# Reading the dense products' columns in woven lines of 16, with operands at new places modulo 512 bytes

## What is computed

```python
def first_block(x, ...):
    h = rmsnorm(x, attn_norm_w)                  # 256 x 1024
    proj = h @ w_in                              # 1024 x 3072
    y = group_rmsnorm(mixers(proj))
    x = x + y @ w_out                            # 1024 x 1024
    g = rmsnorm(x, ffn_norm_w)
    return x + (silu(g @ w_gate) * (g @ w_up)) @ w_down      # d_ff 2816

def second_block(x, ...):
    proj = rms_norm(x, mix_norm_g) @ w_in
    merged = gates0 * (y_a @ w_branch_a) + gates1 * (y_b @ w_branch_b)
    x = x + merged @ w_out
    up = rms_norm(x, ffn_norm_g) @ w_up
    a = causal_depthwise_conv(up[..., :2816], conv_w, conv_b)
    return rms_norm(x + (gelu(a) * up[..., 2816:]) @ w_down, final_norm_g)
```

## The kernel before

| tile | before | after the change |
| --- | --- | --- |
| `raw0`, `raw1`, `raw2` | 128 | 128 |
| `whi0`, `wlo0` | 128 | 128 |
| `whi1`, `wlo1` | 128 | 192 |
| `whi2`, `wlo2` | 128 | 256 |
| `hx` | 128 | 128 |
| `yx` | 160 | 320 |
| `G` | 128 | 128 |

## Time and profile before

### The profile page before, as it was taken

One profiled execution on the slowest core, in us unless ns is written; L12 is line 12 of the kernel. 1 busy time (PEld: TensorE's weight loads), 2 busy tenths in 40 slices (PEclk: granted clock), 3 DMA queues, 4 the chain that ended last, 5 costly groups with the idle time before them and its releaser, 6 DMA issues.

```text
span 689.2 us, 10065 instructions
## 1 busy us (share of the span) xinstructions
PE 681.6 (99%) x4120; PEld 601.0 (87%) x4120; DVE 498.7 (72%) x690; ACT 400.7 (58%) x503; POOL 9.3 (1%) x25
## 2 busy tenths in 40 slices
PE   9999999999999999999999999999999999999996
PEld 8889999888888888888878888899988888888885
DVE  6875777979986766766665477687779988886453
ACT  7875856755555544464467465564557666665342
POOL 1000000003000000000000000000000000000000
PEclk9999999999999999999999999999999999999999
DMA  8853325655565555545434346454555555554611
GB/s 328 337 224 123 117 70 182 222 184 192 184 217 184 201 184 184 186 181 193 175 126 179 123 150 217 153 183 155 184 200 197 192 179 189 193 197 174 222 61 61
DMA packets 19773, 124.05 MB, mean 180 GB/s; under 512 B 2320, under 2 KB 3472, under 8 KB 5520
## 3 DMA queue, kind: packets, MB, share of 16 engines
q1 hardware_dynamic: 18432, 120.07, 49.0%
q10 hardware_dynamic: 1296, 3.35, 1.4%
HBM read 122.36 MB, written 1.05 MB: 179 GB/s over the span
## 4 chain that ended last, share of the span: by engine, by line
PE 91%; DVE 4%; ACT 3%; issue 1%; DVEq 0%; POOL 0%; ACTq 0%; POOLq 0%
PE psum L1628 35%; PE psum L1629 18%; PE psum L1621 10%; PE psum L1622 10%; PE psum L1623 10%; PE psum L1617 2%; DVE wlo L985 2%; ACT whi L530 2%; PE psum L1972 1%; PE psum L2103 1%; PE psum L1671 1%; PE psum L1674 1%; PE psum L1677 1%; PE psum L2151 0%; DVE gates L1522 0%
## 5 line engine op out<-in xcount | busy, mean ns | idle before, releaser
L985 DVE TENSOR_TENSOR wlo<-raw,whi 128x2048 fp32r<-128x2048 f32 x110 | 251.6, 2290 | 75.3 <-ACT whi L530 75.3
L530 ACT CAST whi<-raw 128x2048 fp32r<-128x2048 f32 x110 | 209.7, 1908 | 43.4 <-PE psum L1623 38.1
L1628 PE MATMUL psum<-hx,whi 128*128 128x512 f32 x528 | 184.2, 395 | 0.0
L1629 PE MATMUL psum<-hx,wlo 128*128 128x256 f32 x528 | 146.7, 278 | 0.0
L1628 PE MATMUL psum<-yx,whi 128*128 128x512 f32 x352 | 123.2, 392 | 1.0 <-DVE yx L1001 1.0
L1628 PEld LDWEIGHTS psum<-hx,whi 128*128 128x128 f32 x528 | 99.0, 188 | 23.3 <-issue 0.2
L1629 PEld LDWEIGHTS psum<-hx,wlo 128*128 128x128 f32 x528 | 99.3, 188 | 0.0
L1629 PE MATMUL psum<-yx,wlo 128*128 128x256 f32 x352 | 99.2, 282 | 0.0
L1628 PEld LDWEIGHTS psum<-yx,whi 128*128 128x128 f32 x352 | 66.1, 188 | 15.3 <-DVE yx L1001 1.6
L1629 PEld LDWEIGHTS psum<-yx,wlo 128*128 128x128 f32 x352 | 66.5, 189 | 0.0
L1628 PE MATMUL psum<-G,whi 128*128 128x512 f32 x176 | 61.1, 394 | 0.0
(11 more groups left out here) (273 smaller groups left out, 1106.3 us busy)
## 6 DMA issues: line engine op xcount, KB each, us to landing
raw<-in_stream SPq DMA_DIRECT2D x110, 1024.0 KB, 4.8
raw<-in_stream SPq DMA_DIRECT2D x8, 256.0 KB, 5.3
relb<-in_relb ACTq DMA_DIRECT2D x1, 1536.0 KB, 7.4
raw<-in_stream SPq DMA_DIRECT2D x2, 512.0 KB, 7.4
x<-in_xT SPq DMA_DIRECT2D x3, 256.0 KB, 5.1
out_t<-sq SPq DMA_DIRECT2D x4, 160.0 KB, 2.4
final_gain<-in_final_gain ACTq DMA_DIRECT2D x1, 512.0 KB, 4.8
bsp<-in_bsp ACTq DMA_DIRECT2D x1, 384.0 KB, 3.4
```

The source lines that it names most:

```text
L530: act.copy(whi[s][:], raw[s][:]).then_inc(unit_hi, 1)
L985: dve.tensor_tensor(wlo[s][:], raw[s][:], whi[s][:], ALU.subtract).then_inc(unit_lo, 1)
L1628: pe.matmul(bank[b][:], stat[0], mov, start=first, stop=False, skip_group_check=True)
L1629: return pe.matmul(bank[b][:, 0:T], stat[1], mov[:, 0, :], start=False, stop=last, skip_group_check=True)
```

## The change

Three things change. No instruction is added, removed or moved on any engine: the built programs have 3970 matmuls each, and as many instructions on DVE, ACT, POOL and SP.

First, the dense matmuls read their streamed columns, and write PSUM, in another order. `woven` turns an access to 512 columns (two halves of 256) into 16 rounds of 16 columns of the first half and 16 of the second: columns 0 to 15, 256 to 271, 16 to 31, 272 to 287, and so on. 256 columns are read the same way as two halves of 128 in 8 rounds. The destination is walked in the same order, so each column's sum goes where it went before. Sixteen fp32 columns are 64 bytes. The halves begin 1024 bytes apart (512 bytes for 256 columns). In the last unit, pieces of 384 and 128 columns stay as they were.

Second, the allocation order is another one, with three pads of 64 bytes, so that the weights' three places lie at 128, 192 and 256 modulo 512, `hx` at 128 and `yx` at 320.

Third, `LEAD` is 112 in place of 160, which makes up for the pads: `G` and `gates` stay where they were.

```diff
-LEAD = 160
+LEAD = 112
...
         raw = [sb(f"raw{s}", [P, UNIT]) for s in range(RING)]
-        whi = [sb(f"whi{s}", [P, UNIT], F32R) for s in range(RING)]
-        wlo = [sb(f"wlo{s}", [P, UNIT], F32R) for s in range(RING)]
-
-
+
+
+        whi, wlo = [None] * RING, [None] * RING
+
+        def place(s):
+            whi[s] = sb(f"whi{s}", [P, UNIT], F32R)
+            wlo[s] = sb(f"wlo{s}", [P, UNIT], F32R)
+
+        hx = sb("hx", [P, KT, 2, T], F32R)
+        place(0)
+        sb("before_second", [P, 16])
+        place(1)
+        sb("before_third", [P, 16])
+        place(2)
+        sb("before_yx", [P, 16])
+        yx = sb("yx", [P, KT, 2, T], F32R)
         sq = sb("sq", [P, KT, T])
-        hx = sb("hx", [P, KT, 2, T], F32R)
...
-        yx = sb("yx", [P, KT, 2, T], F32R)
...
+            def woven(ap):
+
+                if len(ap.shape) == 3:
+                    return ap.rearrange("p h (j c) -> p j h c", c=16)
+                if ap.shape[1] % UF:
+                    return ap
+                return ap.rearrange("p (h j c) -> p j h c", h=2, c=16)
+
+            def woven_matmul(dst, stat, mov, **kw):
+                return pe.matmul(woven(dst), stat, woven(mov), **kw)
+
             def three(dst, stat, mov, first, last, **kw):
 
-                pe.matmul(dst, stat[0], mov[0], start=first, stop=False, **kw)
-                pe.matmul(dst, stat[0], mov[1], start=False, stop=False, **kw)
-                return pe.matmul(dst, stat[1], mov[0], start=False, stop=last, **kw)
+                woven_matmul(dst, stat[0], mov[0], start=first, stop=False, **kw)
+                woven_matmul(dst, stat[0], mov[1], start=False, stop=False, **kw)
+                return woven_matmul(dst, stat[1], mov[0], start=False, stop=last, **kw)
 
             def tiles(b, stat, mov, first, last):
 
 
-                pe.matmul(bank[b][:], stat[0], mov, start=first, stop=False, skip_group_check=True)
-                return pe.matmul(bank[b][:, 0:T], stat[1], mov[:, 0, :], start=False, stop=last, skip_group_check=True)
+                woven_matmul(bank[b][:], stat[0], mov, start=first, stop=False, skip_group_check=True)
+                return woven_matmul(bank[b][:, 0:T], stat[1], mov[:, 0, :], start=False, stop=last, skip_group_check=True)
```

More of the change, by code:

```diff
@@ L1670, in first_unit @@
                     for t, c in enumerate(tokens):
-                        pe.matmul(bank[6 + t][:], hh[:, k, c], whi[u][:, w], start=k == 0, stop=False)
+                        woven_matmul(bank[6 + t][:], hh[:, k, c], whi[u][:, w], start=k == 0, stop=False)
                     pe.wait_ge(*((unit_lo, u + 1) if last else (piece_lo, pieces_before(u) + 1 + kk)))
                     for t, c in enumerate(tokens):
-                        pe.matmul(bank[6 + t][:], hh[:, k, c], wlo[u][:, w], start=False, stop=False)
+                        woven_matmul(bank[6 + t][:], hh[:, k, c], wlo[u][:, w], start=False, stop=False)
                     pe.wait_ge(h_lo, k + 1)
                     for t, c in enumerate(tokens):
-                        ins = pe.matmul(bank[6 + t][:], hl[:, k, c], whi[u][:, w], start=False, stop=k == KT - 1)
+                        ins = woven_matmul(bank[6 + t][:], hl[:, k, c], whi[u][:, w], start=False, stop=k == KT - 1)
                         if k == KT - 1 and t == 0:
```

## The result

The change makes the kernel slower: 713.26 us (713.16 to 714.27) against 691.1, a ratio of 1.032 with a 95% interval of 1.031 to 1.033. I had forecast 667, with 652 to 701 as the range. The sign is wrong, and the time lies outside the range.

What follows compares the result with a forecast made beforehand. PE's matmul pace was taken to bound the kernel: 24.7 us gained by the weave less 0.7 us of new waits, net -24.0 from 690.96, gives 666.96, stated as 667 us; range 652 to 701, likeliest case 652 to 680.

Steps and rivals of the forecast that it cites:

- What bounds the kernel: PE, busy 681.6 of 689.2 us with next to no holes; time is the number of matmuls times their pace.
- the cover: DVE and ACT staying ahead of a faster PE; 0.7 us of new PE waits, between 0 and 3.
- the reading of the excess: Dense matmuls: about 13.2 ns over their columns, from the next weight load meeting the current stream; 47.0 us in all.
- nothing changes: Rival: the excess is the cost of switching weights, which no read order touches; 691 us, chance 0.10.
- The argument about two walkers of one speed: Woven stream walks 512 bytes in 107 ns, about the load's speed; from different starts the two need not meet.
- The term of the weave: All 3660 dense matmuls: excess falls to 6.1 ns, a gain of 24.7 us, between 10.8 and 38.6.
- the line change costs a cycle: Rival: every dense product pays 0.417 ns a line, 36.0 us in all; 703 or 727 us; slower had chance 0.20.
- places only: Rival: the weave gains little and new tile places give a small gain; 684 us, 680.2 to 689.7, chance 0.14.
- other tiles shift, at no cost: Pads and new allocation order shift other tiles by up to 192 bytes, costed at nothing.

Runs made afterwards that it cites:

- sixteen_fewer: Kernel before the change, with the second matmul of each straight group of three streaming 16 columns fewer; 689.08 us.
- half_load: Kernel before the change, with the second matmul of each straight three and the wlo matmul of each tiles pair loading 64 of 128 weight columns; 691.68 us.
- write_woven: Kernel before the change, with PSUM written in woven lines of 16 columns and the streamed operand read straight; 690.62 us.

## Why the prediction was wrong

**What bounds the kernel** was read rightly: PE is the line that sets the time, and a nanosecond per dense matmul is 3.66 us. Of the 24.3 us by which the dense distances grew, 22.3 came through in the span. Nothing on DVE, ACT or the queues mattered, and the cover (0.7 us of new waits) wasn't called on.

**The step that failed is the reading of the excess** as a meeting of the weight load with the stream. It stood on two observations: equal excess at 256 and 512 columns, and 116.6 against 120.0 ns at two places. The first is half true. The products of three have 13.3 ns at either width (9.9 with `yx`), but in the pairs, the commonest form, 13.2 is only the mean of 18.3 ns at 512 columns and 8.3 at 256 (231.6 and 115.0 ns in the gauge; the starts in the earlier trace rows, 0.23 and 0.11 us apart, hinted at it). Where it is equal it is as good for a fixed cost of each matmul, which I had listed under "nothing changes" with a chance of 0.10 at most; `sixteen_fewer` speaks for that at 512 columns past `G`, and `half_load` against the meeting there; at 256 columns neither run fits either reading. The second is real, but the place isn't all there is to it: the same distance gives 346.7 or 353 ns a pair by what ran before. The argument about two walkers of one speed had nothing firmer under it. The page of the Trainium skill that I set against the trace ("TensorE: Matmul & The Clock Gate", Part 2), by which loading the next weights takes no bandwidth from the running matmul, isn't contradicted by `half_load` at 512 columns: 230.5 ns beside a load of 64 columns, 231.6 beside one of 128. I had it refuted on too little.

**The term of the weave** was put at -24.7 us, between -38.6 and -10.8. It measured +22.0 (713.15 against 691.13). Both ends of my range for it were gains, since I took them from rows of straight reads alone. The trace had no row with a stepped access at all; I said so, and gave the step's own price to a rival in place of widening the term. That was the second mistake: a cost that no row shows belongs in the main sum with both signs.

**The rival "the line change costs a cycle"** is what came, in substance: the excess grows with the columns, 26.7 ns at 512 and 13.3 at 256, as I had written it would. Its numbers were off. It had one cycle a line on top of the straight excess (727), or with the forecast gain (703). Measured is two cycles a line of 16, but in place of the straight 13.3 ns and not on top. For 512 columns that is 64 cycles in place of 32; for 256 it is 32 in place of 32, which is why the products of three with 256 columns of `hx` lost nothing. That it is two cycles is so for lines of 16 alone; the other lengths have other prices. It also named SBUF and PSUM together; PSUM has no part in it. The Trainium skill's statement, in "PSUM — Partial Sum Buffer" under its specifications, that any non-contiguous pattern slows matmuls significantly, isn't borne out for runs of 64 bytes: `write_woven` took 690.62 us.

**The rival "places only"**, a gain at 684, has the wrong sign: the places alone took 696.96, a loss of 5.8 us, and under the weave they did nothing. The part "other tiles shift, at no cost" holds as far as it can be seen: DVE's and ACT's busy times are the same to 1 us.

**The chances**: 0.70 for faster against 0.20 for slower. With a fixed cost per matmul at its proper weight, and the step priced from both sides, slower would have been at least even.

## What to carry to other kernels

Let the streamed operand of an fp32r matmul run in contiguous pieces of 64 columns or more: 64 were free here, 32 cost 13.7 us. Steps in the PSUM access were free at 64 bytes, so if a layout has to be exchanged, exchange it on the PSUM side. Look at the excess by shape before averaging it over a pair. Where it is equal for two sizes, a fixed cost is the first reading, and one run that shortens the suspected partner tests a meeting before anything is built on it. And where the trace has no row of the kind that a change introduces, its price has two signs in the sum itself.

## What the runs showed of the hardware

- An fp32r stream whose read access steps every 16 columns takes 240.0 and 120.0 ns for 512 and 256 columns, 18 cycles of 2.4 GHz for 16 columns, whatever the tiles' places and the distance between lines (0, 768 or 1024 bytes at 512 columns), and within 0.4 ns also beside a weight load of half the size. Lines of 32 columns take 237.8 ns at 512 in the pairs, lines of 8 take 241.7, and lines of 64 are the straight read.
- A woven write into PSUM in lines of 16 columns costs nothing: 579 matmuls in 100 us, as before.
- A straight fp32r matmul of 512 columns past `G`, with its own weight load and at the places of before, takes 13.3 ns more than its columns once the sequence has settled. After a change of shape it takes up to 236 ns in place of 227 for some five matmuls, and at other places up to 233.3. At 256 columns 113.3, 116.7 and 120 ns all occur.
- The same pair of shapes at the same places modulo 512 runs at 346.7 or at 353.2 ns, within one kernel.
- Left open: what the 13.3 ns are, why the step's cost isn't linear in the number of steps, how the length of the weight load moves the 256-column products, and what carries the phase from unit to unit.
